# A two-branch decoder layer on one core: layer norm 1 applied before or after the first four steps of FFN up

## The reference

```python
x = layer_norm(DEEPNORM_ALPHA * x + merged @ W['w_out'][l], W['ln1_g'][l], W['ln1_b'][l])
gate_ff, up_ff = jnp.split(x @ W['w_ffn_up'][l], 2, axis=-1)
x = layer_norm(DEEPNORM_ALPHA * x + (jax.nn.silu(gate_ff) * up_ff) @ W['w_ffn_down'][l], W['ln2_g'][l], W['ln2_b'][l])

def layer_norm(x, g, b):
    xf = x.astype(jnp.float32)
    mu = jnp.mean(xf, axis=-1, keepdims=True)
    var = jnp.mean(jnp.square(xf - mu), axis=-1, keepdims=True)
    return ((xf - mu) * lax.rsqrt(var + LN_EPS) * g + b).astype(x.dtype)
```

## Time and profile before

| | us |
|---|---|
| median of 3 runs | 1766.19 (1764.98 to 1766.56) |
| the profiled execution | 1767.19 |
| its span, first to last instruction | 1765.1 |
| PE busy | 1714.8 (97%) |
| DVE busy | 1038.2 (59%) |
| ACT busy | 791.7 (45%) |
| mean granted TensorE clock | 0.990 |

### The profile page before, as it was taken

How to read it: one execution, slowest core, us unless ns; L and a number is a source line. 1 busy time by engine, 2 the same in 40 slices (tenths; PEclk the granted TensorE clock), 3 DMA queues, 4 the chain that set the end, 5 groups by cost and what they waited for, 6 DMA issues and landing times.

```text
span 1765.1 us, 33323 instructions
## 1 busy us (share of the span) xinstructions
PE 1714.8 (97%) x13826; PEld 1661.1 (94%) x13826; DVE 1038.2 (59%) x1240; ACT 791.7 (45%) x878; POOL 23.6 (1%) x47
## 2 busy tenths in 40 slices
PE   6999999999999999999997999999999999999995
PEld 6999989899999999999997999999999999999995
DVE  7877788666657545455577444444444444454655
ACT  4455544466544444444345444434344443333433
POOL 1000000000010000000000000000000000000000
PEclk9999999999999999999998999999999999999998
DMA  7565567876757887666554555555555555555552
GB/s 223 145 194 164 155 187 233 247 215 208 221 152 238 275 252 235 188 180 180 179 171 128 163 177 180 179 178 178 179 179 178 178 179 182 180 180 179 180 178 75
DMA packets 309117, 329.63 MB, mean 187 GB/s; under 512 B 12175, under 2 KB 289939, under 8 KB 308756
## 3 DMA queue, kind: packets, MB, share of 16 engines
q1 hardware_dynamic: 306736, 325.36, 59.8%
q10 hardware_dynamic: 2276, 2.76, 0.4%
HBM read 322.31 MB, written 5.77 MB: 186 GB/s over the span
## 4 chain that ended last, share of the span: by engine, by line
PE 93%; DVE 4%; ACT 1%; DMA 1%; issue 1%; SPq 0%; ACTq 0%; DVEq 0%
PE ps L648 15%; PE ps L1007 15%; PE ps L1006 14%; PE ps L1008 14%; PE ps L649 14%; PE ps L650 14%; PE ps L738 1%; PE ps L718 1%; PE ps L876 1%; DVE w_split L1441 1%; DMA w_in_ring<-in_w_in 1%; PE ps L686 0%; PE ps L697 0%; DMA w_in_ring<-in_w_out 0%; PE ps L664 0%
## 5 line engine op out<-in xcount | busy, mean ns | idle before, releaser
L2122 DVE TENSOR_TENSOR w_lo<-w_raw,w_hi 128x1024 fp32r<-128x1024 f32 x264 | 323.0, 1225 | 366.1 <-ACT w_hi L1355 364.6
L648 PE MATMUL ps<-xh,w_split 128*128 128x264 f32 x1680 | 486.9, 290 | 16.4 <-DVE w_split L1441 16.3
L1441 DVE TENSOR_TENSOR w_split<-w_in_ring,w_split 128x1024 fp32r<-128x1024 f32 x276 | 338.0, 1228 | 261.9 <-ACT w_split L1067 253.2
L1355 ACT ACTIVATE w_hi<-w_raw 128x1024 fp32r<-128x1024 f32 x264 | 279.7, 1061 | 454.3 <-PE ps L1008 449.5
L649 PE MATMUL ps<-xl,w_split 128*128 128x264 f32 x1680 | 479.7, 286 | 0.0
L650 PE MATMUL ps<-xh,w_split 128*128 128x264 f32 x1680 | 479.1, 285 | 0.0
L1067 ACT ACTIVATE w_split<-w_in_ring 128x1024 fp32r<-128x1024 f32 x276 | 290.8, 1059 | 358.5 <-DMA w_in_ring<-in_w_in 265.2
L1006 PE MATMUL ps<-xh,w_hi 128*128 128x264 f32 x1408 | 403.5, 287 | 11.4 <-DVE xl L2173 11.4
L1007 PE MATMUL ps<-xl,w_hi 128*128 128x264 f32 x1408 | 404.1, 287 | 0.0
L1008 PE MATMUL ps<-xh,w_lo 128*128 128x264 f32 x1408 | 403.2, 286 | 0.0
L648 PEld LDWEIGHTS ps<-xh,w_split 128*128 128x128 f32 x1680 | 319.0, 190 | 39.9 <-issue 29.5
(11 more groups left out here) (422 smaller groups left out, 1614.5 us busy)
## 6 DMA issues: line engine op xcount, KB each, us to landing
w_in_ring<-in_w_in SPq DMA_DIRECT2D x210, 512.0 KB, 3.7
w_raw<-in_w_ffn_up SPq DMA_DIRECT2D x176, 512.0 KB, 3.6
w_raw<-in_w_ffn_down SPq DMA_DIRECT2D x88, 512.0 KB, 3.3
kv<-in_cache_k SPq DMA_DIRECT2D x64, 258.0 KB, 3.8
w_in_ring<-in_w_branch SPq DMA_DIRECT2D x32, 512.0 KB, 3.4
kv<-in_cache_v SPq DMA_DIRECT2D x64, 256.0 KB, 3.8
w_in_ring<-in_w_out SPq DMA_DIRECT2D x32, 512.0 KB, 3.3
x_t<-in_x SPq DMA_DIRECT2D x8, 264.0 KB, 8.3
```

The lines of the kernel that those rows point to most:

```text
L648: nc.tensor.matmul(out, w_split[:, slot, 0, c], right_h[:, k, :], start=first, stop=False)
L1355: A_(w_hi[:, n % RING2, :], raw[:, n % RING2, :], ACT.Copy).then_inc(sem("hi2"), 1)
L1441: V.tensor_tensor(w_split[:, slot, 1, :], w_in_ring[:, slot, 1, :], w_split[:, slot, 0, :], ALU.subtract).then_inc(sem("lo_done"), 1)
L2122: V.tensor_tensor(w_lo[:, n % RING2, :], raw[:, n % RING2, :], w_hi[:, n % RING2, :], ALU.subtract).then_inc(sem("lo2"), 1)
```

## The change

FFN up's first four steps (`Z_STEPS = 4`, chunks up 0 to up 31) no longer take the normalized `x1`. They take z = residual times ln1_g, split into `xh` and `xl`, and so can run before mean and deviation are known. `xh` and `xl` get two more columns (264 and 265) that hold ln1_g and ln1_b; the matmuls of these steps have 266 columns, so that each product also carries W·g and W·b. With these, gate = (W z - mean · W g) / deviation + W b, which DVE (`normal`) and ACT (`silu_z`) apply to each product. The sums of layer norm 1 stand on PE after up 2. The values `x1` are still made, in steps 1 and 2 (`x1_norm` on DVE, `x1_values` on ACT), split in step 4 (`x1_high`, `x1_low`), and used from step 4 on and by the second residual. Steps 0 to 4 are written out, the loop has steps 5 to 21.

```diff
-X1_TILES = [(0, 1), (1, 2), (2, 4), (4, 6), (6, 8), (8, 12), (12, 16)]
+Z_STEPS = 4
...
+    xh = place("xh", [P, KT, TOK + 2], F32R, at_xh)
+    xl = place("xl", [P, KT, TOK + 2], F32R, at_xl)
...
         until(END - 1)
-        layer_sums(0, xp[:, KT - 2:KT, :])
...
+        for i in range(Z_STEPS):
             for j in range(8):
+                if i == 0 and j < 4:
+                    pe.wait_ge(sem("z_low"), 2 * (j + 1))
+                up_chunk(i, j, TOK + 2)
+                if i == 0 and j == 2:
+                    pe.wait_ge(*told("acc_all", 1))
+                    sums("l_mu", 0, acc_d, 2)
+                    sums("l_var", 0, acc_q, 2)
+        for j in range(8):
+
+            if j < 4:
+                pe.wait_ge(sem("x1_low"), j + 1)
+            up_chunk(Z_STEPS, j)
+        with nc.tensor.Fori(Z_STEPS + 1, UP_STEPS) as i:
...
             for m in range(7):
                 if n == last_chunk(pass_of("out", m, 0)) + (12 if m == 0 else 9 if m == 1 else 5):
                     squares(0, m, xp)
+                    z_high(m)
...
+        def z_high(m):
+
+            for t in (2 * m, 2 * m + 1):
+                ins = A_(xh[:, t, 0:TOK], xp[:, t, :], ACT.Copy, scale=lnv[:, 0, t:t + 1])
+            ins.then_inc(sem("z_high"), 1)
...
         squares(0, 6, xp)
-        steps.do(A_(small[:, 63:64], ones[:, 0:1], ACT.Sqrt))
+        z_high(6)
         squares(0, 7, xp)
+        z_high(7)
+        highs(C_UP + 4, C_UP + 7)
         deviation(0)
...
+        def silu_z(i):
+            act.wait_ge(*told("z_gate", i + 1))
+            for t in range(2):
+                ins = A_(sg[:, t, :], sg[:, t, :], ACT.Silu, bias=small[:, 2 * t + 1:2 * t + 2])
+            ins.then_inc(sem("sg_z"), 1)
...
+        def x1_values(m):
+
+            act.wait_ge(*told("x1_norm", m + 1))
+            for t in (2 * m, 2 * m + 1):
+                ins = A_(x1[:, t, :], xp[:, t, :], ACT.Identity, scale=lnv[:, 0, t:t + 1], bias=lnv[:, 1, t:t + 1])
+            ins.then_inc(sem("x1_done"), 1)
...
+        silu_z(0)
+        for i in range(1, Z_STEPS + 1):
+            for j in range(8):
+                highs(8 * i + j, 8 * i + j + 1)
+                if i in (1, 2) and 3 <= j < 7:
+                    x1_values(4 * (i - 1) + j - 3)
+                if i == Z_STEPS and j < 4:
+                    x1_high(j)
+                if j == 5:
+                    h_high_z(i - 1)
+            if i < Z_STEPS:
+                silu_z(i)
...
                     squares_added(0, m)
+                    z_low(m)
+
+        def z_low(m):
+
+            dve.wait_ge(sem("z_high"), m + 1)
+            for t in (2 * m, 2 * m + 1):
+                ins = V.scalar_tensor_tensor(xl[:, t, 0:TOK], xp[:, t, :], lnv[:, 0, t:t + 1], xh[:, t, 0:TOK], ALU.mult, ALU.subtract)
+            ins.then_inc(sem("z_low"), 1)
...
+        residual(0, 7, xp)
+        squares_added(0, 6)
+        z_low(6)
 
         dve.wait_ge(*used(END - 2))
         lows(0, 2)
...
+        def normal(dst, col, p, i):
+
+
+            own = small[:, col:col + 4].rearrange("p (t c) -> p t c", c=2)
+            dve.wait_ge(sem("used2"), i * 8 + 4 * (p - pg) + 4)
+            then(V.tensor_copy(own, PS[:, BANK(p):BANK(p) + 2, TOK:TOK + 2]))
+            do(V.scalar_tensor_tensor(dst[:, 0, :], mu_r[:, 0, :], small[:, col:col + 1], PS[:, BANK(p), 0:TOK],
+                                      ALU.mult, ALU.subtract))
+            V.scalar_tensor_tensor(dst[:, 1, :], mu_r[:, 0, :], small[:, col + 2:col + 3], PS[:, BANK(p) + 1, 0:TOK],
+                                   ALU.mult, ALU.subtract).then_inc(sem(f"evac{p % 2}"), 1)
+            steps.settle()
+            dve.wait_ge(sem(f"evac{p % 2}"), i + p // 2 + 1)
+            then(V.tensor_tensor(dst[:, :, :], dst[:, :, :], minus_r[:, :, :].to_broadcast([P, 2, TOK]), ALU.mult))
...
+        def x1_norm(m):
+            shifted(xp, 2 * m, 2 * m + 2)
+            scaled(xp, 2 * m, 2 * m + 2, "x1_norm")
...
+        gate_z(0)
+        for i in range(1, Z_STEPS + 1):
+            for j in range(8):
+                lows(8 * i + j, 8 * i + j + 1)
+                if j == 2:
+                    h_product_z(i - 1)
+                if j == 6:
+                    h_low_z(i - 1)
+                if i in (1, 2) and 3 <= j < 7:
+                    x1_norm(4 * (i - 1) + j - 3)
+                if i == Z_STEPS and j < 4:
+                    x1_low(j)
+            if i < Z_STEPS:
+                gate_z(i)
+        with nc.vector.Fori(Z_STEPS + 1, UP_STEPS) as i:
```

More of the change, by code:

```diff
@@ L647, in chunk @@
                     c = slice((kk * tiles + half) * P, (kk * tiles + half) * P + P)
-                    nc.tensor.matmul(out, w_split[:, slot, 0, c], right_h[:, k, :], start=first, stop=False)
-                    nc.tensor.matmul(out, w_split[:, slot, 0, c], right_l[:, k, :], start=False, stop=False)
-                    ins = nc.tensor.matmul(out, w_split[:, slot, 1, c], right_h[:, k, :], start=False, stop=last)
+                    nc.tensor.matmul(out, w_split[:, slot, 0, c], right_h[:, k, 0:TOK], start=first, stop=False)
+                    nc.tensor.matmul(out, w_split[:, slot, 0, c], right_l[:, k, 0:TOK], start=False, stop=False)
+                    ins = nc.tensor.matmul(out, w_split[:, slot, 1, c], right_h[:, k, 0:TOK], start=False, stop=last)
             ins.then_inc(sem("used"), 1)
@@ L2104, in _ @@
             tell(dve, "empty_f_o", 1)
+        dve.wait_ge(sem("lnv_loaded"), 16)
+        for n in range(2):
+            then(V.tensor_copy(xh[:, :, TOK + n], lnv[:, n, :]))
+            do(V.tensor_tensor(xl[:, :, TOK + n], lnv[:, n, :], xh[:, :, TOK + n], ALU.subtract))
+        then(V.memset(small[:, 62:63], LN_EPS))
         weights(V_AT[15] + 5)
@@ L2137, in scaled, with layer_norm @@
             tell(dve, name, 1)
-        def layer_norm(n, src, p, ready, between):
+        def layer_norm(n, src, p, ready):
             out_pass(n, 7, p, ready, src)
-            between()
             dve.wait_ge(*made("l_mu", n + 1))
@@ L2154, in layer_norm @@
             then(V.reciprocal(mu_r[:, 1, :], mu_r[:, 1, :]))
-        then(V.memset(small[:, 62:63], LN_EPS))
+        residual(0, 7, xp)
+        squares_added(0, 6)
+        z_low(6)
         dve.wait_ge(*used(END - 2))
         lows(0, 2)
-        residual(0, 7, xp)
-        squares_added(0, 6)
+        out_pass(0, 7, pass_of("out", 7, 0), used(END - 1), xp)
+        lows(2, 3)
+        squares_added(0, 7)
         tell(dve, "acc_all", 1)
-        def last_lows():
-            dve.wait_ge(*used(END - 1))
-            lows(2, 4)
@@ L2188, in _ @@
-        x1_low(6)
-        lows(C_UP + 5, C_UP + 8)
-        pg, pu = P_UP, P_UP + 1
+        z_low(7)
+        lows(3, 6)
+        dve.wait_ge(*made("l_mu", 1))
+        then(V.tensor_scalar(mu_r[:, 0, :], PS[:, banks("l_mu", 0)[0], 0:TOK], 1.0 / D_MODEL, None, ALU.mult))
+        tell(dve, "empty_l_mu", 1)
+        then(V.tensor_tensor(mu_r[:, 1, :], mu_r[:, 0, :], mu_r[:, 0, :], ALU.mult))
+        dve.wait_ge(*made("l_var", 1))
+        then(V.scalar_tensor_tensor(mu_r[:, 1, :], PS[:, banks("l_var", 0)[0], 0:TOK], 1.0 / D_MODEL, mu_r[:, 1, :],
+                                    ALU.mult, ALU.subtract))
@@ L2193, in h_product, with gate_z, h_product_z @@
+        def gate_z(i):
+            normal(sg, 0, pg, i)
+            tell(dve, "z_gate", 1)
+        def h_product_z(i):
+            if i:
+                dve.wait_ge(sem("hl_done"), i)
+            normal(hx, 4, pu, i)
+            dve.wait_ge(sem("sg_z"), i + 1)
+            for t in range(2):
+                do(V.scalar_tensor_tensor(hx[:, t, :], hx[:, t, :], small[:, 5 + 2 * t:6 + 2 * t], sg[:, t, :], ALU.add, ALU.mult))
+            steps.settle()
+            tell(dve, "hx_z", 1)
         def h_product(i, hh_count):
```

129 lines of the change are left out of this document (57 added, 72 removed).

## The result

| | us |
|---|---|
| kernel after, median of 6 runs | 1772.94 (1769.07 to 1773.33) |
| kernel before, median of 6 runs beside it | 1765.95 (1763.94 to 1766.56) |
| ratio after / before | 1.0037, 95% interval 1.0027 to 1.0047 |
| forecast | 1766.5, range 1761 to 1773 |
| the profiled execution, its span | 1773.25, 1771.0 |

The changed kernel is 0.37% slower, at the upper edge of the range. The case that I gave 0.55 put it at no change, so most of the loss is not in the sum. The page of after shows first where it is not: PE is as full as before and bounds the kernel still. The lines are busy time by engine, and the chain that ended last by engine; they answer to the earlier trace rows.

What follows compares the result with a forecast made beforehand. PE, busy 97% of the span, was taken to bound the kernel. Removed 21.8 us and added 21.6 net -0.2, a median of 1766.0; 0.5 for the clock makes 1766.5 us, range 1761 to 1773.

Steps and rivals of the forecast that it cites:

- The case that I gave 0.55: Whole kernel: the forecast's own sum, 1766.5 us, with its terms off by up to 3 us either way; chance 0.55.
- the rows at nothing: PE's reads of `xh` and `xl`: rows of 1064 instead of 1056 bytes cost nothing, with 0 to 9 us as bounds.
- What goes: Layer norm 1: step 0's waits for x1, slow stretches and two of four groups of sums go, 21.8 us removed.
- Term 1: Out stage: z's low and high parts ahead of the splits make PE stall at out 19, 2.7 us added.
- Term 2: First chunk of FFN up: z's last parts delay the low part of up 0, PE stalls 2.3 us.
- Term 3: FFN up's first 32 chunks: two more columns in each of 768 matmuls, 0.6 us added.
- Term 4: Steps 1 and 2: ACT and DVE take turns over x1 at 5.0 us a chunk, PE stalls 16 us.
- The clock: Steps 1 and 2: the clock may fall in both places, 3.5 us before cover, mostly hidden; 0.5 us kept.
- (b): Steps 1 and 2: the clock stays down through both bursts of stalls, not hidden, 1772.8 us; chance 0.22 in whole or part.
- Rival (a): Steps 1 and 2: the turn-taking of ACT and DVE is hidden, 1750.5 us; chance 0.15 in whole or part.
- Rival (d): Start of FFN up: up 0 still waits for the statistics, so the hole stays, 1782 us; chance 0.02.
- Rival (c): PE's reads of `xh` and `xl`: rows of 1064 bytes slow them, up to 9 us, 1775 us; chance 0.06.

Runs made afterwards that it cites:

- b_row1064: Kernel before with only the rows of `xh` and `xl` lengthened from 1056 to 1064 bytes: 1771.71 us, ratio to before 1.0036.
- a_out: Kernel after with z's parts spread later over the out stage and the low parts of up 0 and up 1 moved earlier: 1766.15 us, ratio to before 0.9998.
- a_turn: Kernel after with ACT making each pair of x1's values one chunk later, behind the next chunk's high part: 1760.81 us, ratio to before 0.996.
- a_row1072: Kernel after with rows of `xh` and `xl` of 1072 bytes instead of 1064: 1760.23 us, ratio to before 0.9963.
- b_shift64: Kernel before with `xh` and `xl` both moved by 64 bytes, their distance unchanged: 1766.48 us beside 1766.62 of before, one execution each.
- b_row1072: Kernel before with rows of `xh` and `xl` of 1072 bytes instead of 1056: 1759.04 us, ratio to before 0.9953.

## Why the prediction was right where it was, and where not

The time fell in the range by 0.06 us, which is luck: its distance from the forecast has a cause to which I gave a chance of 0.06. The case of 0.55 was right about the changed part and wrong about the kernel.

- **The step that failed: the rows at nothing.** I took no cost for rows of 1064 bytes because the nearest matmuls showed none wherever their tile lay, and kept 0 to 9 us as bounds. Measured alone: 5.3 us (b_row1064), inside the bounds of 0 to 9, but I had put it at 0. Rows of 2064 bytes under 128 x 512 matmuls spread from 592 to 617 ns, and that spread of 4% was itself the hint: a 0.5% shift fits in it many times. "No row excludes it" was the right thing to write and 0.06 too small for it.
- **What goes: 21.8 us.** Right as far as the trace shows. All waits for x1 in step 0 and both slow stretches went.
- **Term 1, out 19, 2.7 us.** The place was right, the idle time 2.21 (2.4 from start to start). What was missing is the clock, which fell right there for another 1.6; no wait stood behind it to cover that. Measured 4.0. a_out shows that the stall came from the parts of z ahead of the splits.
- **Term 2, up 0, 2.3 us.** Measured 1.84 idle, 2.0 from start to start.
- **Term 3, two columns, 0.6 us.** From the paces of the 266- and 264-column matmuls of after, 123.7 and 123.0 ns, 768 x 0.7 = 0.5. With rows of 1072 bytes the same two columns cost more, 123.4 against 121.1, 1.8 us. No run tells why.
- **Term 4, 16 us.** Seven stalls, as forecast, ended by low parts of chunks. The mechanism is shown by a_turn. The reserves, which the forecast called its weakest place, were right: 4.5 us ahead of up 11 (forecast 4.7) and 2.7 ahead of up 19 (2.8). The round was too long: 4.76 instead of 5.0, and from the low part of up 11 (983.29) to that of up 16 (1008.55) it is 25.3 instead of 26.6. From up 11 to up 16 PE lost 6.1 us (forecast 7.0), from up 19 to up 24 7.8 (9.0): 13.9 in all. The idle time in the lines above is less, 9.3, because PE spent a part of the lost time on slow matmuls.
- **The clock, 0.5 us.** The reason was right, the size too small. The clock fell four times, three of them within the turn-taking. Two of these falls, in up 15 and up 22, were covered, as I had argued: the chunk went through slowly and PE still waited behind it for DVE (0.39 at 1009.92, 0.75 at 1036.44). The turn-taking itself didn't notice. The low parts from up 11 to up 16 start 4.77, 4.76, 5.30, 5.38 and 5.03 us apart in after, and 4.77, 4.77, 5.30, 5.38 and 5.04 in a_row1072, where the clock didn't fall between up 1 and up 16. The third fall stood in up 24, behind the last stall, and PE lost 1.6 us by it. That is the case which I had named under (b), PE at half pace after the last stall, and had not put into the sum. Term 4 with its clock is 13.9 + 1.6 = 15.5 against 16.5: an error of 2.1 and one of 1.1 that cancel in part. It is also what a_turn took away: from up 11 to up 26 after needs 60.1 us and a_turn 44.6.
- **The sum of the part.** Added 4.0 + 2.0 + 0.5 + 15.5 = 22.0, removed 21.8: net +0.2, forecast +0.3. The traces say the same: the stretch from out 15 to up 47 grew by 1.1 us, of which 0.7 is the pace.
- **Rival (a)**, hidden turn-taking: fell, as the stalls show. **Rival (b)**, the clock down through a burst for 10 us: didn't come in that form; short falls did. **Rival (d)**: fell; PE starts up 0 at 954.49 and makes the sums of layer norm 1 only behind up 2, which starts at 960.54. **Rival (c)**: came, with 5.3 of its up to 9 us, and moved the time to the upper edge of the range.

The sign for (c) that I gave, a pace over 0.123 before 850, looked at the right place, but as a threshold it was poor: in the stretch from 300 to 600 us before has 300 / 2439 = 0.1230 us a matmul and after 0.1237. It works only as a comparison of the two.

## What to carry to other kernels

Before costing a change, ask of every buffer whose rows or place it alters how many instructions read it: 0.5 ns on each of some 9,000 matmuls cost more than the whole reordering as it was written, and it shows as a count of matmuls in an untouched stretch in which PE is full. When two in-order engines hand work to each other in both directions, put the item that the other one needs next ahead of the one that must wait for it; one position in ACT's program was worth 12 us. And judge a change together with repairs that its trace names: the same idea was 0.4% slower as written and 1.6% faster with three small edits.

## What the runs showed of the hardware

- **The place of an operand in SBUF changes the pace of fp32r matmuls.** Matmuls of 264 columns with a weight load each, in FFN up: 122.5 ns with rows of 1056 bytes, 123.05 with 1064, 121.4 with 1088, 121.1 with 1072, 121.7 with 1056 and `xl` 64 bytes further on. It is the same to 0.01 us a step for kernels with the same placement, and tile by tile it repeats with a period of 256 bytes (before against b_shift64).
- **The clock fell behind single idle gaps of 1.8 to 2.2 us, and the length of the gap alone doesn't tell whether it falls.** In after it fell behind one idle gap of 2.21 us (912.65), where PE had been nearly full at full clock since 600 us, and didn't fall behind the single gap of 1.84 us (954.49). In a_row1072 it fell behind the same gap of 1.84 us at up 0 (946.88). In b_row1072 it fell behind the gap of 1.92 us ahead of the sums (943.05), which before has too (947.49) without a fall. The stretches behind these gaps, of a_row1072 and then of b_row1072:

```profile
946.88:950.36 3.48, 3.48 (x16) 3.48 (x17) 3.30 (x4) 1.57 (x3) 0.00 (x0) 0.51 0.67 181
943.05:946.60 3.55, 3.55 (x9) 2.73 (x10) 3.01 (x3) 0.64 (x1) 0.00 (x0) 0.53 0.49 146
```

The Trainium skill ("TensorE: Matmul & The Clock Gate", section "Why this matters for your kernels") names only longer idle gaps than these as what brings the clock down. This trace disagrees: from 600 us on the longest wait of PE in after is 2.21 us, and the clock fell four times.
